# Ends of three projections in a two-block transformer kernel: two places for the next weights, the last tile of tokens by halves of the width

## The reference

```python
mix = concatenate([y_conv, y_ret]) @ w_out            # rows "out", depth 1024
x = x + gate1 * rms_norm(mix, g_post_mix)
h = rms_norm(x, g_pre_mlp) * (1.0 + scale2) + shift2  # boundary "out"
f = square(relu(h @ w_fc1)) @ w_fc2                   # rows "fc2", depth 4096
x = x + gate2 * rms_norm(f, g_post_mlp)
u = rms_norm_2(x, norm_g[0]) @ pool_w_in              # boundary "fc2"
...
h = h + (m * silu(gate)) @ pool_w_out                 # rows "pout", depth 2048
u = rms_norm_2(h, norm_g[1]) @ hgrn_w_in              # boundary "pout"
...
h = h + (o * silu(gate)) @ hgrn_w_out                 # rows "hout"
return rms_norm_2(h, final_g)
```

## Time and profile before

| | us |
|---|---|
| median of 3 runs | 1491.99 (1491.56 to 1494.17) |
| the profiled execution | 1491.2 |
| its span | 1489.4 |
| PE busy in the span | 1448.1 |
| DVE busy | 872.6 |
| ACT busy | 564.4 |

### The profile page before, as it was taken

How to read it: one execution, slowest core, us unless ns; L and a number is a source line. 1 busy time by engine, 2 the same in 40 slices (tenths; PEclk the granted TensorE clock), 3 DMA queues, 4 the chain that set the end, 5 groups by cost and what they waited for, 6 DMA issues and landing times.

```text
span 1489.4 us, 18491 instructions
## 1 busy us (share of the span) xinstructions
PE 1448.1 (97%) x7204; PEld 1205.4 (81%) x7204; DVE 872.6 (59%) x1718; ACT 564.4 (38%) x1025; POOL 0.2 (0%) x4
## 2 busy tenths in 40 slices
PE   4999999999999999999999999999999999999998
PEld 4788887888888887888888887888888888888786
DVE  7786766553333334756467334425778877787545
ACT  5423345422232223543333224333444434444332
POOL 0000000000000000000000000000000000000000
PEclk9999999999999999999999999999999999999999
DMA  8645551363332233123223332332222221222221
GB/s 330 216 147 214 178 170 55 99 214 97 100 95 92 96 99 113 58 99 110 89 85 114 99 97 78 110 98 80 64 69 72 72 68 61 71 72 69 73 71 58
DMA packets 43863, 158.31 MB, mean 106 GB/s; under 512 B 4864, under 2 KB 5248, under 8 KB 43776
## 3 DMA queue, kind: packets, MB, share of 16 engines
q1 hardware_dynamic: 43776, 157.12, 32.4%
HBM read 155.00 MB, written 2.10 MB: 105 GB/s over the span
## 4 chain that ended last, share of the span: by engine, by line
PE 90%; DVE 5%; ACT 3%; DMA 1%; issue 1%; SPq 0%; ACTq 0%; DVEq 0%
PE PS L470 28%; PE PS L472 27%; PE PS L471 27%; PE PS L756 1%; PE PS L804 1%; PE PS L767 1%; PE PS L808 1%; PE PS L798 1%; PE PS L776 1%; PE PS L784 1%; DVE RAW L921 1%; DMA X<-in_x 1%; DVE WL L951 1%; PE PS L823 1%; DVE X L1066 1%
## 5 line engine op out<-in xcount | busy, mean ns | idle before, releaser
L470 PE MATMUL PS<-HH,WH 128*128 128x512 f32 (+1 forms) x1152 | 452.2, 393 | 4.5 <-ACT TMP L1747 2.4
L472 PE MATMUL PS<-HH,WL 128*128 128x512 f32 (+1 forms) x1152 | 437.7, 380 | 0.0
L471 PE MATMUL PS<-HL,WH 128*128 128x512 f32 (+1 forms) x1152 | 436.5, 379 | 0.0
L951 DVE TENSOR_TENSOR WL<-RAW,WH 128x1024 fp32r<-128x1024 f32 x225 | 273.8, 1220 | 79.8 <-ACT WH L1648 79.5
L1648 ACT ACTIVATE WH<-RAW 128x1024 fp32r<-128x1024 f32 x225 | 237.1, 1057 | 186.7 <-PE PS L472 147.7
L470 PEld LDWEIGHTS PS<-HH,WH 128*128 128x128 f32 x1152 | 218.3, 190 | 43.6 <-issue 3.7
L472 PEld LDWEIGHTS PS<-HH,WL 128*128 128x128 f32 x1152 | 218.0, 189 | 42.0
L471 PEld LDWEIGHTS PS<-HL,WH 128*128 128x128 f32 x1152 | 218.7, 190 | 37.0 <-issue 1.0
L470 PE MATMUL PS<-WH,ZH 128*128 128x512 f32 x400 | 155.6, 389 | 0.0
L472 PE MATMUL PS<-WH,ZL 128*128 128x512 f32 x400 | 155.6, 389 | 0.0
L471 PE MATMUL PS<-WL,ZH 128*128 128x512 f32 x400 | 155.6, 389 | 0.0
(11 more groups left out here) (248 smaller groups left out, 1648.9 us busy)
## 6 DMA issues: line engine op xcount, KB each, us to landing
RAW<-in_w_fc SPq DMA_DIRECT2D x64, 512.0 KB, 3.5
RAW<-in_hgrn_in SPq DMA_DIRECT2D x64, 512.0 KB, 3.5
RAW<-in_ada SPq DMA_DIRECT2D x43, 512.0 KB, 4.5
RAW<-in_pool_in SPq DMA_DIRECT2D x40, 512.0 KB, 3.5
RAW<-in_w_in SPq DMA_DIRECT2D x27, 512.0 KB, 4.1
RAW<-in_pool_out SPq DMA_DIRECT2D x16, 512.0 KB, 3.5
RAW<-in_hgrn_out SPq DMA_DIRECT2D x16, 512.0 KB, 3.5
RAW<-in_w_out SPq DMA_DIRECT2D x8, 512.0 KB, 4.1
```

What stands on the lines that cost most here:

```text
L470: e.matmul(out, wh, xh, start=first, stop=False)
L471: e.matmul(out, wh, xl, start=False, stop=False)
L472: return e.matmul(out, wl, xh, start=False, stop=last)
L951: e.tensor_tensor(lo, raw(i), hi.bitcast(F32), ALU.subtract).then_inc(taken.sem, taken(i))
```

## The change

Four edits, in the three boundaries:

- Units 0 and 1 of w_fc1, pool_in and hgrn_in get two places of their own in parts of Z (`NS + NE + n`). Their high and low parts are made at the end of `rows` (`hi_to(end + NE)`, `lo_to(end + NE)`), before the boundary's first step. The ring of four then starts with unit 2. `normal` and `gated` move to other parts of Z to make room.
- In `rows` on PE the last tile is made half by half: all six kept units for n = 0, then all six for n = 1. The first transposes stand after the second kept unit of n = 0. For "hout" the last tile was made in this way before.
- In `halved` on PE the second transposes move from ahead of k = 6 to ahead of k = 7.
- In `boundary` the steps of the last tile are cut in halves (`take`, `out_square`), and `highs` and `lows` of the first transposes are spread around them. On DVE `lows` 0 to 3 stand ahead of the last tile's steps, 4 and 5 behind them, 6 behind the split of unit 3, and 7 behind `token_factors(stage, 2, 2)` and `normed_tokens(stage, 3)`. On ACT `highs` 4 and 5 stand behind the last tile's second square, 6 and 7 behind the sum of squares of its new X.

```diff
--- before.py
+++ after.py
@@ -66,6 +66,8 @@
         if (name in ("w_out", "w_fc2", "pool_out") and n >= LENGTH[name] - NE
                 or name == "hgrn_out" and n in (8, 9, 14, 15)):
             slot = NS + n % 2
+        elif name in ("w_fc1", "pool_in", "hgrn_in") and n < NE:
+            slot = NS + NE + n
         else:
             slot = ring % NS
             ring += 1
...
@@ -285,18 +287,22 @@
 
             if SLOT[s] < NS:
                 return WH[:, SLOT[s], :], WL[:, SLOT[s], :]
-            base = (8 if UNITS[GEMM[s]][0] in ("w_out", "w_fc2") else 16) + 4 * (SLOT[s] - NS)
+            if SLOT[s] < NS + NE:
+                base = (8 if UNITS[GEMM[s]][0] in ("w_out", "w_fc2") else 16) + 4 * (SLOT[s] - NS)
+            else:
+                base = {"w_fc1": (4, 20), "pool_in": (24, 28), "hgrn_in": (8, 12)}[UNITS[GEMM[s]][0]][
+                    SLOT[s] - NS - NE]
             return tuple(ZR[:, i:i + 2, :].rearrange("p a b -> p (a b)") for i in (base, base + 2))
 
         def normal(stage, t):
 
             if stage == "x":
                 return flat(8 + 2 * t if t < 3 else 16)
-            return flat((24 if stage == "pout" else 16) + 2 * t)
+            return flat(24 + 2 * t if stage == "pout" else 16 + 2 * (t % 2))
 
         def gated(stage, t):
 
-            return flat((0 if stage == "out" else 24) + 2 * (t % 2))
+            return flat((0 if stage == "out" else 20) + 2 * (t % 2))
 
         def z_place(z):
 
...
@@ -508,11 +514,11 @@
                     for u in range(4):
                         if q == 0:
                             next_unit()
-                        if q == 0 and u == 3:
-                            transposed(stage, 1)
                         hi, lo = place(first + u)
                         wh, wl = (x.rearrange("p (k c) -> p k c", k=2) for x in (hi, lo))
                         for kk in range(2):
+                            if q == 0 and u == 3 and kk == 1:
+                                transposed(stage, 1)
                             k, half = 2 * u + kk, slice(256 * q, 256 * q + 256)
                             e.wait_ge(*ready(stage, q, k))
                             for j in (2 * q, 2 * q + 1) if tokens else range(4):
...
@@ -578,9 +584,7 @@
                             m = product(s, k, t, n)
                     m.then_inc(read.sem, read("w", s))
                     wfree[s] = zfree[base + k] = read.sem, read.n
-                for t in range(4):
-                    if stage == "hout" and t == 3:
-                        break
+                for t in range(3):
                     for i in range(STAY):
                         k, s = nk - STAY + i, kept + i
                         if t == 0:
...
@@ -591,19 +595,19 @@
                             m = product(s, k, t, n)
                             if k == nk - 1:
                                 m.then_inc(banks.full[b], banks.fill((stage, t, n), b))
-                        if t == 3 and k < nk - 1:
+
+                for n in range(2):
+                    b = out_bank(stage, 3, n)
+                    for i in range(STAY):
+                        k, s = nk - STAY + i, kept + i
+                        m = product(s, k, 3, n)
+                        if k == nk - 1:
+                            m.then_inc(banks.full[b], banks.fill((stage, 3, n), b))
+                        elif n == 1:
                             m.then_inc(read.sem, read("w", s))
                             wfree[s] = zfree[base + k] = read.sem, read.n
-                        if t == 3 and i == 3 and stage != "hout":
+                        if n == 0 and i == 1 and stage != "hout":
                             transposed(stage, 0)
-                if stage == "hout":
-
-                    for n in range(2):
-                        b = out_bank(stage, 3, n)
-                        for i in range(STAY):
-                            m = product(kept + i, nk - STAY + i, 3, n)
-                        m.then_inc(banks.full[b], banks.fill((stage, 3, n), b))
-                    return
                 wfree[s] = zfree[base + k] = banks.made((stage, 3, 1))
 
 
...
@@ -1009,6 +1013,7 @@
                     if k + 2 < nk:
                         z_low(k + 2, base + k + 2)
                     lo_to(min(p.unit + (3 if k >= nk - STAY - 1 else 2), end))
+                lo_to(end + NE)
 
             def root(to, n):
 
...
@@ -1050,13 +1055,19 @@
                 e.tensor_scalar(normal(stage, t), X[:, t, :], RT[:, t:t + 1], None, ALU.mult).then_inc(
                     own.sem, own("normed", stage, t))
 
+            def take(stage, t, n):
+
+                b, c = out_bank(stage, t, n), slice(512 * n, 512 * n + 512)
+                if stage in ("out", "fc2"):
+                    e.wait_ge(square.sem, square.of(stage, t, n))
+                    e.tensor_tensor(gated(stage, t)[:, c], PS[b][:, :], G[:, c], ALU.mult).then_inc(banks.free[b], 1)
+                else:
+                    e.wait_ge(*banks.made((stage, t, n)))
+                    e.tensor_tensor(X[:, t, c], X[:, t, c], PS[b][:, :], ALU.add).then_inc(banks.free[b], 1)
+
             def add_normed(stage, t):
 
                 y = gated(stage, t)
-                for n in range(2):
-                    b, c = out_bank(stage, t, n), slice(512 * n, 512 * n + 512)
-                    e.wait_ge(square.sem, square.of(stage, t, n))
-                    e.tensor_tensor(y[:, c], PS[b][:, :], G[:, c], ALU.mult).then_inc(banks.free[b], 1)
                 e.scalar_tensor_tensor(out=NW[:, 4, 0:1], in0=SSY[:, 2 * t:2 * t + 1], scalar=EPS,
                                        in1=SSY[:, 2 * t + 1:2 * t + 2], op0=ALU.add, op1=ALU.add).then_inc(
                                            own.sem, own())
...
@@ -1065,12 +1076,6 @@
                 e.wait_ge(own.sem, own.n)
                 e.scalar_tensor_tensor(out=X[:, t, :], in0=y, scalar=R1[:, t:t + 1], in1=X[:, t, :],
                                        op0=ALU.mult, op1=ALU.add).then_inc(tdone.sem, tdone(stage, "x", t))
-
-            def add(stage, t):
-                for n in range(2):
-                    b, c = out_bank(stage, t, n), slice(512 * n, 512 * n + 512)
-                    e.wait_ge(*banks.made((stage, t, n)))
-                    e.tensor_tensor(X[:, t, c], X[:, t, c], PS[b][:, :], ALU.add).then_inc(banks.free[b], 1)
 
             def lows(stage, q, tiles, gain):
 
...
@@ -1090,20 +1095,26 @@
 
             def boundary(stage, gain):
 
-                tile, s = (add if stage == "pout" else add_normed), p.unit
-                tile(stage, 0)
-                tile(stage, 1)
-                token_factors(stage, 0, 2)
-                tile(stage, 2)
-                lo_to(s + 1)
+                s = p.unit
+                for t in range(3):
+                    take(stage, t, 0)
+                    take(stage, t, 1)
+                    if stage != "pout":
+                        add_normed(stage, t)
+                    if t == 1:
+                        token_factors(stage, 0, 2)
                 lows(stage, 0, range(4), gain)
-                lo_to(s + 2)
-                lows(stage, 0, range(4, 8), gain)
+                take(stage, 3, 0)
                 lo_to(s + 3)
-                tile(stage, 3)
+                take(stage, 3, 1)
+                if stage != "pout":
+                    add_normed(stage, 3)
+                lows(stage, 0, (4, 5), gain)
                 lo_to(s + 4)
+                lows(stage, 0, (6,), gain)
                 token_factors(stage, 2, 2)
                 normed_tokens(stage, 3)
+                lows(stage, 0, (7,), gain)
                 lows(stage, 1, range(8), gain)
 
 
...
@@ -1643,7 +1654,7 @@
                     e.wait_ge(*landed(i))
                     if BEFORE[s] is not None:
                         e.wait_ge(*wfree[BEFORE[s]])
-                    if SLOT[s] == NS:
+                    if SLOT[s] in (NS, NS + NE):
                         e.wait_ge(*spare(UNITS[i][0]))
                     e.activation(place(s)[0], raw(i), ACT.Copy).then_inc(whi.sem, whi(s))
 
...
@@ -1655,6 +1666,8 @@
                     return zlo.sem, zlo.of(8 + 15)
                 if name == "pool_out":
                     return banks.taken(("pm", 3, 3))
+                if name in ("w_fc1", "pool_in", "hgrn_in"):
+                    return zlo.sem, zlo.of({"w_fc1": 7, "pool_in": 39, "hgrn_in": 55}[name])
                 return banks.taken(("ho", 15))
 
             def walk(n):
...
@@ -1724,6 +1737,7 @@
                     if k + 2 < nk:
                         z_high(k + 2, base + k + 2, there)
                     hi_to(min(p.unit + (4 if k >= nk - STAY else 3), end))
+                hi_to(end + NE)
 
             def token_squares(stage, t):
 
...
@@ -1775,15 +1789,14 @@
 
                 s = p.unit
 
-                def out_squares(t):
+                def out_square(t, n):
                     if stage != "pout":
```

(30 more changed lines are left out.)

8 lines of the change are left out of this document (4 added, 4 removed).

## The result

The kernel after takes 1500.13 us (median; 1496.86 to 1502.53), beside 1491.93 us for the kernel before on the same chip (1490.96 to 1494.17). The ratio is 1.0052, with an interval of 1.0038 to 1.0066: the change makes the kernel 8.2 us slower, and 1499.3 was predicted. The profiled execution took 1499.84 us, its span 1498.1, which is 8.7 more than the 1489.4 before.

The account below looks back on a forecast made before the run. PE, busy 1448.1 of 1489.4 us, was taken as the bound, so only its idle or low-clock time counts. 0.0 ("out") + 6.5 ("fc2") + 0.8 ("pout") = +7.3 us gave a median of 1499.3; range 1495.8 to 1503.0.

Parts of the forecast that it names:

- Out: Boundary w_out to w_fc1: bank 3's product at 256.95, first whole column at 282.2 against 282.16 before, so 0.0 us.
- one low stretch of 1.47: In the boundary from w_out to w_fc1: 16 matmuls at the 1.2 GHz level, 1.47 us, as in the earlier trace.
- Fc2: Boundary where DVE reads bank 3: its product at 623.45, first whole column at 648.7 against 642.21, so +6.5 us.
- The waits forecast: In the "fc2" boundary, PE waits 5 us ahead of nine matmuls and 2 to 3 us for DVE behind them.
- The mis-sized term: Clock in "fc2": one low stretch, 1.47 us, taken as the nearest row; bounds were none or two stretches.
- rival B: Clock in "out" and "fc2": two low stretches in each stall, 1502.2 us in all; chance 0.12.
- Pout: Boundary claiming only banks 0 and 1 at first: first matmul at 930.5 against 929.72, +0.8 us; nothing later is late.
- The edits put at nothing: Early splits of units 0 and 1, and the restructured `take`/`add_normed` with the "hout" halves: 0 us each.
- Rival D: Early splits push tile 0's chain past tile 1's square: about +1 us in one or two boundaries, 1500.8; chance 0.06.
- Rival A: In the three boundaries, bank 3's claim costs nothing and PE goes straight on: together -10.9 us, 1481.1; chance 0.12.

## Why the prediction was right

It was right by its own steps but for the size of one term.

**"Out".** Bank 3's product was predicted at 256.95 - 239.95 = 17.00 us after the tile's start and came at 255.80 - 238.83 = 16.97. From there the prediction has 9.05 us to the second transposes and one low stretch of 1.47; the trace has 266.43 - 255.80 = 10.63, so 1.58 for the clock. The sum 0.0 came out as 0.08. The nine matmuls stand between the two waits (2.56 and 1.74 us) as written.

**"Fc2".** Bank 3 was predicted 20.30 us after the tile's start and came at 20.12. The waits forecast were 5 us ahead of nine matmuls and 2 to 3 behind them; they were 4.93 ahead and 1.82 behind, just short of that, since a wait of 0.34 for bank 2 (f = 6) falls among the nine and they ran low themselves. The releaser and the queue in front of it are as written.

**The mis-sized term** is the clock in "fc2". One stretch of 16 matmuls, 1.47 us, was taken from the earlier trace rows. Behind bank 3's wait 26 matmuls ran at the low level. From bank 3's product to the second transposes it is 633.82 - 622.21 = 11.61 us for the 9.05 of the full clock, so 2.56 for the clock. (The nine ahead of that wait ran low too and cost nothing: the wait was long enough to hold them.) So the seam lost 7.37 instead of 6.5: +1.1 by the clock, -0.18 by the chain. The size of this term was not in any row: "fc2" before had one low stretch of its own, about as long as that of "out", and the kernels here with nearly the same first wait have 13 to 35 low matmuls. Filling the waits with matmuls gave back 2.5 us in "fc2" and 1.5 in "out", which is the same split by another way. This is a part of rival B: nearly two low stretches, but in one boundary of the two. It was rightly kept as a case, and the range (up to 1503.0) holds it. That the median came within 0.9 us of the forecast is partly luck, as the two stretches outside the boundaries (-1.12 and +1.67) and the spread of the runs (1496.86 to 1502.53) are larger than that.

**"Pout".** +0.75 against +0.8, its first wait 1.27 us against 1.3.

**The edits put at nothing.** The places cost nothing: with the places alone the kernel takes the same time (0.9993); with the reads early they are worth some 3 us. Rival D had the early splits delaying tile 1's squares. Tile 1's second square in "fc2" starts 7.86 us ahead of the last tile's first matmul in both (594.23 and 602.09 after, 595.29 in the earlier trace rows and 603.15 before). The cover shrank from 1.88 us to 0.40, as the splits took from it, and it held.

```profile
593.45 0.60 ACT L1797 ACTIVATE TMP<-PS 128x512 f32<-128x512 f32 x1 [0.40 <-PE PS L478]
...
594.23 0.60 ACT L1797 ACTIVATE TMP<-PS 128x512 f32<-128x512 f32 x1
```

**Rival A** named the faster case rightly: that it hangs on whether f = 7 is read before the last tile's chain ends. Reading f = 7 a little earlier was not enough (1494.78 us, with f = 4 to 6 still behind the last tile's steps). With all the reads put ahead of these steps, the kernel took 1480.72 us, where A's sum was 1481.1, with -6.9, -3.9 and -0.7 in the three boundaries for -6.6, -3.8 and -0.5. All other edits of the change are good for 11 us, and the position of the reads in two queues takes 19.

**What stays open.** The stretch ahead of "out" (-1.12) and what follows the first matmul of "pout" (+1.67) make up 0.55 us of the difference in span. Of the second, 1.63 us arise behind a wait near the end that both kernels have (below). For the first no cause was looked for; over the profiles here that start varies by 3.5 us. The medians of the whole kernel don't resolve parts under some 2 us, so the worth of the moved transposes is known from the trace alone.

## What to carry to other kernels

When reads of PSUM are moved down in an engine's queue, look up the instruction of PE that claims the last bank they free, not only the one that uses the values read: here the value of f = 7 was wanted some 12 us later than its bank (268.09 and 255.80 in after's "out"). The same goes for f = 4 to 6 and banks 0 to 2. Spreading work around a chain saved that chain nothing here and held the busiest engine for the length of it. And a stretch of low clock or a wait is worth removing only where nothing waits behind it that would take in the gain: the low stretches of the kernel before in these boundaries were free.

## What the runs showed of the hardware

**The same wait isn't always followed by the low clock.** Far behind the change, in the recurrent layer, PE waits 1.43 us for DVE in both kernels (L771 after, L767 before). The kernel after went on at the low level, the one before didn't. The rows of PE and the window, first of after:

```profile
1401.92 1.16 PE L771 MATMUL PS<-Z 128*128 128x64 f32 x8 [1.43 <-DVE Z L1518]
...
1402.84 0.78 PE L476 MATMUL PS<-WH,HH 128*128 128x512 f32 x1
```

```profile
1402.80:1407.00 4.20, 4.20 (x14) 3.36 (x13) 1.29 (x5) 0.00 (x0) 0.00 (x0) 0.60 0.43 125
```

and of before:

```profile
1394.85 1.07 PE L767 MATMUL PS<-Z 128*128 128x64 f32 x8 [1.43 <-DVE Z L1507]
...
1395.73 0.48 PE L470 MATMUL PS<-WH,HH 128*128 128x512 f32 x1
```

The clock is 0.60 in the one (1.00 in the like window of before), and the matmul lasts 0.78 us and not 0.48. From the L771 row to the end of the span it is 96.18 us after and 94.55 before, +1.63, which is nearly all that was lost behind "pout"; the change moves no instruction there. The other way round, a longer wait of the kernel before, 3.18 us early in the span, was followed by a window at 1.00:

```profile
47.19 0.47 PE L470 MATMUL PS<-WH,HH 128*128 128x512 f32 x1 [3.18 <-DVE HL L1132]
```

```profile
47.20:50.60 3.40, 3.40 (x15) 2.85 (x16) 1.96 (x3) 3.13 (x5) 0.00 (x0) 1.00 1.03 412
```

So the length of a wait alone doesn't tell the level. Different kernels show it too: in "fc2" 35 (after), 13 (DVE's `lows` 7 moved), 27 (ACT's copy moved as well) and 23 (bank 3 claimed last) matmuls ran low, and their first waits are all 4.92 or 4.93 us; the second and third of these have the same order on DVE.

The Trainium skill ("TensorE: Matmul & The Clock Gate", section "What's actually happening") says that the number of slow matmuls at the start of a kernel changes from run to run of the same kernel. Only one run of each kernel has a trace here, so no count shows it; but the runs agree in kind, within a kernel and not at its start: the 11 runs with bank 3 claimed last have mean granted clocks from 0.992 (1496.28 and 1497.46 us) to 0.997 (1491.05 us).

**Matmuls that compute nothing hold the clock.** With the waits filled it stayed at 1.00, and the two seams were 4.0 us shorter, although bank 3's products started as late as before the filling (16.98 and 20.13 us after the tile's start).

**The transposes are slowed as well** where they begin at the low level: 16 of them in 3.38 us for 1.91 to 1.94.

**The start of the kernel varies.** The last tile of "out" begins between 238.74 and 242.19 us over the profiles of the kernels with the two places, with nothing ahead of it changed. Only differences within a seam, or medians of several runs, can be set against the change.
